# The order in which a decoder kernel's tensors lie in an SBUF partition

## What is computed

```python
def block(xb):                       # tokens; 8 heads, k = 16, 16384 experts a layer
    q = (xb @ w_query).reshape(tb, PEER_HEADS, 2, PEER_KEY_DIM // 2)
    s = jnp.einsum('thpd,pnd->thpn', q, sub_keys)
    top_s, top_i = lax.top_k(s, k)
    cand_s = top_s[:, :, 0, :, None] + top_s[:, :, 1, None, :]
    ...
    gate = jax.nn.softmax(best_s, axis=-1)
    u = expert_u[idx]
    act = jax.nn.gelu(jnp.einsum('thkd,td->thk', u, xb))
    w = (gate * act)
    return jnp.einsum('thk,thkd->td', w, expert_v[idx])
```

## The kernel before

| tensor | bytes | starts before | starts after |
|---|---|---|---|
| h, hn, hT | 12288 each | 128 | 0 |
| gain, qT, skT, con | 4096, 8192, 2048, 2632 | 128 | 0 |
| wring | 32768 | 224 | 0 |
| arena | 77824 | 224 | 0 |
| gws | 40512 | 224 | 96 |
| small | 256 | 288 | 128 |
| g1w, rows512, onorm, feat_cols | 512, 2048, 1024, 88 | 32 | 160 |
| top | 128 | 128 | 384 |
| top_i, top_f, pairs and what follows | | unchanged | unchanged (pairs 0) |

## Time and profile before

### The profile page before, as it was taken

One profiled execution on the slowest core, in us unless ns is written; L12 is line 12 of the kernel. 1 busy time (PEld: TensorE's weight loads), 2 busy tenths in 40 slices (PEclk: granted clock), 3 DMA queues, 4 the chain that ended last, 5 costly groups with the idle time before them and its releaser, 6 DMA issues.

```text
span 1687.8 us, 13940 instructions
## 1 busy us (share of the span) xinstructions
PE 1402.9 (83%) x4006; PEld 672.1 (40%) x4006; DVE 1110.3 (66%) x2844; ACT 426.0 (25%) x1115; POOL 553.7 (33%) x582
## 2 busy tenths in 40 slices
PE   8999799799887779798788769797788878777785
PEld 7744454264333334343335324343335333333332
DVE  1233565767777786766867687776867677777764
ACT  1132122222332223321222223321222222222221
POOL 0023232234333332232433333242433434333331
PEclk9989899899999989899999989898999998999998
DMA  7500579999999999999999999999999999999994
GB/s 260 204 1 1 223 300 412 409 375 383 419 420 419 420 393 379 360 413 390 419 410 417 413 390 413 413 409 379 420 409 418 405 417 420 420 419 421 419 414 198
DMA packets 107953, 617.11 MB, mean 366 GB/s; under 512 B 10939, under 2 KB 11195, under 8 KB 40294
## 3 DMA queue, kind: packets, MB, share of 16 engines
q0 software_dynamic: 76032, 553.68, 80.1%
q1 hardware_dynamic: 31846, 62.53, 10.1%
HBM read 615.13 MB, written 1.05 MB: 365 GB/s over the span
## 4 chain that ended last, share of the span: by engine, by line
PE 46%; DMA 31%; DVE 12%; issue 6%; ACT 2%; POOL 1%; DVEq 0%; SPq 0%; POOLq 0%
DMA arena<-peer_uv,idx 31%; PE bank L1061 24%; PE bank L688 9%; DVE arena L1834 3%; PE bank L727 3%; PE bank L1036 3%; ACT arena L1393 1%; PE bank L857 1%; PE bank L877 1%; POOL arena L637 1%; DVE wgt L1855 1%; DVE pairs L1758 1%; DVE top_i L1768 1%; DVE top_i L1759 0%; DVE h L1840 0%
## 5 line engine op out<-in xcount | busy, mean ns | idle before, releaser
L1061 PE MATMUL bank<-arena 128*128 128x512 f32 x1944 | 956.8, 641 | 243.2 <-ACT arena L1393 220.3
L1834 DVE CUSTOM_DVE_ANT_0 arena<-arena,bank 128x1024 f32<-128x1024 f32 x528 | 639.7, 1219 | 369.7 <-DMA arena<-peer_uv,idx 366.1
L637 POOL DMA_INDIRECT arena<-peer_uv,idx x528 | 513.6, 973 | 946.0 <-PE bank L1061 907.5
L1061 PEld LDWEIGHTS bank<-arena 128*128 128x128 f32 x1944 | 381.7, 204 | 770.9 <-issue 743.9
L1393 ACT ACTIVATE arena<-con,wgt 128x128 f32<-128x128 f32 x486 | 170.7, 394 | 751.4 <-DVE wgt L1855 736.3
L688 PE MATMUL bank<-wring,hT 128*128 128x512 f32 x368 | 162.9, 596 | 0.0
L1382 ACT ACTIVATE gl<-dots 128x2 f32<-128x2 f32 x264 | 53.6, 203 | 284.8 <-DVE dots L1834 279.2
L688 PEld LDWEIGHTS bank<-wring,hT 128*128 128x128 f32 x368 | 70.8, 193 | 89.5 <-issue 89.5
L1855 DVE SCALAR_TENSOR_TENSOR wgt<-gate_e,z,gl 128x2 f32<-128x2 f32 x264 | 57.5, 218 | 25.6 <-ACT gl L1382 19.5
L1840 DVE SCALAR_TENSOR_TENSOR h<-arena,wgt,h 128x1024 f32<-128x1024 f32 x42 | 54.0, 1285 | 1.7 <-DVE wgt L1855 0.2
L1382 ACT ACT_TABLE_LOAD x39 | 50.0, 1283 | 0.7
(11 more groups left out here) (209 smaller groups left out, 899.5 us busy)
## 6 DMA issues: line engine op xcount, KB each, us to landing
wring<-gla_w_in SPq DMA_DIRECT2D x12, 2048.0 KB
arena<-peer_uv,idx POOLq DMA_INDIRECT x528
wring<-gla_w_out SPq DMA_DIRECT2D x4, 2048.0 KB
wring<-peer_w_query SPq DMA_DIRECT2D x4, 2048.0 KB
wring<-attn_w_by_tile SPq DMA_DIRECT2D x3, 2048.0 KB
gws<-peer_w_query SPq DMA_DIRECT2D x2, 2048.0 KB, 13.6
wring<-attn_w_out_by_pair SPq DMA_DIRECT2D x2, 2048.0 KB
hn<-uq_by_kind SPq DMA_DIRECT2D x1, 1152.0 KB, 16.7
```

The costliest lines, as they stand in the source:

```text
L637: nc.gpsimd.indirect_dma_start(out=uvrow[:, n % RING, :], out_offset=None, in_=io["peer_uv"].rearrange("l e d -> (l e) d"), in_offset=bass ...
L1061: last = nc.tensor.matmul(yacc[:, 512 * i:512 * i + 512], wdiag[:, k % DIAGS, :], rows_of(g, k, 1)[:, 512 * i:512 * i + 512], start=first, ...
L1834: v.tensor_tensor_reduce(out=rows, in0=rows, in1=xnow, scale=1.0, scalar=0.0, op0=ALU.mult, op1=ALU.add, accum_out=dots[:, g % 2, k:k + 1] ...
```

## The change

Four tensors are declared first: `small` (256 bytes) and `top` (128), which together fill the 384 bytes up to a multiple of 512, then `arena` and `wring`. The rest follows in its old order. No instruction, DMA, wait or size is changed, and each tensor keeps its name and use.

```diff
+        small = sb("small", [P, 64])
+        top = sb("top", [P, 2, TOPK])
+        arena = sb("arena", [P, RING * 2 * D + DIAGS * P])
+        wring = sb("wring", [P, WSLOTS, KC * 512])
         h = sb("h", [P, NB, D])
         hn = sb("hn", [P, NB, D])
         hT = sb("hT", [P, KC, ROWS])
@@
         con = sb("con", [P, LIVE_CONSTS])
-        wring = sb("wring", [P, WSLOTS, KC * 512])
-        arena = sb("arena", [P, RING * 2 * D + DIAGS * P])
         gws = sb("gws", [P, 10128])
-        small = sb("small", [P, 64])
         g1w = sb("g1w", [P, KC, RANK])
@@
-        top = sb("top", [P, 2, TOPK])
         top_i = sb("top_i", [P, 2, TOPK], U32)
```

## The result

The changed kernel takes 1669.86 us (median of six runs, 1666.24 to 1673.69), the kernel before in the same sessions 1691.86 us (six runs): a ratio of 0.9873, 95% interval 0.9855 to 0.989, so 22 us less. The profiled execution took 1667.05 us, its span is 1664.9 us.

A forecast was written before the change was run, and what follows sets the result against it. DMA engines, busy throughout 240 to 1665 us, bound the kernel: startup, bytes over rate, short tail. All terms 0, so 1689.6 us plus 0, given as 1691 beside the runs' median; range 1672 to 1698.

The forecast's parts named there:

- rival B: Saturated gathers: the start costs 4.4 ns a row; 426 GB/s instead of 420, 15 us less, 1676 us; chance 16%.
- Step 1: Gathers' 8192-byte packets into arena: moving their start from 224 to 0 saves nothing; bounds -4.4 and +4.4 ns a row.
- straight line: DMA packets of 2048 to 8192 bytes at 224 or 128: 38 ns per KB plus a constant of 7.1 to 8.1 ns.
- comparison by rate: Packet times from GB/s of single-size stretches: constants at 224 and 128 differ by 0.3 ns, so alignment was put at 0.
- comparison with the aligned sub-keys: Startup sub-key load, 256-byte pieces at 0: 7.8 ns above payload against 10.4 for 2048-byte packets; alignment worth at most 2.6 ns.
- The first gathers: Gathers from 187 to 189 us, few queued: 426 GB/s, 307.7 ns a row against 312.1 saturated; difference laid to saturation.
- Step 2: 20 weight loads in the bound stretch, 1280 packets an engine: taken as 0, bounds -3.3 and +3.3 us.
- Rival A: DMA packets: bytes below the start cost like payload, 8.3 ns a gathered row; -38 us, 1653 us; chance 5%.
- cap of 435 GB/s: DMA ports: the skill page's ceiling would cap any gain of a saturated stretch at 3.4% of 420.
- Rival C: DMA writes meeting engines' accesses at the same place: slower, +4.4 ns a gathered row, +18 us, 1709 us; chance 8%.
- Rival D: Tensor placement: the change does not align, arena at another odd place; time the same, within the forecast, no separate chance.
- Steps 3, 4 and 5: Startup loads, VectorE's operands and PE's moving operands: 0 each; bounds 1.6 us for startup, 2.6 us for VectorE.

The follow-up runs named there:

- arena_only: Kernel before with only arena moved to 0 mod 512; wring and gws stay at 224, h to con at 128: 1673.5 us, ratio 0.9879.
- all_at_256: Changed kernel with arena, wring and h to con moved to 256 mod 512: 1669.3 us, ratio 0.9853 to the kernel before.
- wring_only: Kernel before with only wring moved to 0 mod 512; arena and gws stay at 224, h to con at 128: 1685.2 us, ratio 0.9961.
- all_at_32: Changed kernel with arena, wring and h to con moved to 32 mod 512: 1691.8 us, ratio 1.001 to the kernel before.
- rest_only: Kernel before with only h, hn, hT, gain, qT, skT and con moved to 0 mod 512: 1691.4 us, ratio 0.9995.
- gws_too: Changed kernel with gws at 0 mod 512 as well, con behind it: 1670.89 us, ratio 0.9876 to the kernel before.
- source_and_all_at_32: Changed kernel with arena, wring and h to con at 32 mod 512, and the weights' HBM rows 32 bytes past a multiple of 256: 1693.0 us, ratio 0.9996.
- all_at_64: Changed kernel with arena, wring and h to con moved to 64 mod 512: 1686.7 us, ratio 0.9967 to the kernel before.

## Why the prediction was wrong

The forecast, no change at 1691 us, failed, and the range ended at 1672, 2 us above the median. The mechanism is that of rival B, which had 16%: under pressure the start costs a few nanoseconds a row.

*Step 1, the gathers' packets, is where it fell: "It doesn't follow the start".* The straight line through the earlier trace rows was read rightly, but it could only exclude a price that grows with the bytes between boundary and start. A price that is the same for 224 and for 128 goes into the constant, and there it was, since all four sizes compared started off the boundary. The term for a row was put at 0, and it is 5.1 ns: from 240 us on the 8192-byte packets take 318.1 ns on the mean before and 313.0 in the changed kernel, and 4080 x 5.1 = 21 us. By rate it is the same. Rows at 427 GB/s (arena_only and all_at_256; the changed kernel has 425 to 428) are 8192 x 16 / 427 = 307.0 ns instead of 312.1, 5.1 less, and 2048-byte rows from 12 to 16 us are 79.9 ns at 410 GB/s instead of 84.7 at 387, 4.8 less. So about 5 ns for a packet, whatever its size from 2 to 8 KB, is the price of a start off 256 bytes. With 38 ns per KB taken off, the constants of aligned packets are 3.0 and 3.9 ns, where those of before are 8.1 and 8.7.

*The comparison with the aligned sub-keys* was the one that pointed right. By duration it had 7.8 ns above payload for an aligned packet and 10.4 for one at 224. In the changed kernel the 2048-byte packets from 12 to 16 us all take 84 ns, which is 8 above payload, so the 7.8 was good. The 2.6 ns between them was called the most that alignment could be worth and then put at 0, in favour of the comparison by rate, which had no aligned packet in it. And 2.6 was itself a mean over unlike parts. In the earlier trace rows I had taken 7 to 16 us as one stretch at 393 GB/s. Its two ends, in the kernel before:

```profile
DMA packets 590, 1.21 MB, mean 403 GB/s; under 512 B 0, under 2 KB 0, under 8 KB 590
...
DMA packets 756, 1.55 MB, mean 387 GB/s; under 512 B 0, under 2 KB 0, under 8 KB 756
```

The rate from 7 to 10 us says little by itself: over the profiles with 2048-byte loads it lies between 369 and 409 GB/s, whatever wring's start (382 in the changed kernel, 403 in wring_only). The packets' durations say more. Before, their median is 84 ns from 7 to 10 us, 86 from 10 to 12 and 88 from 12 to 16; in the changed kernel it is 84 throughout. So the extra time was not there at first, and the mean over the stretch hid part of it.

*The first gathers* were a sign of the same kind: 307.7 ns at the same start of 224 was put down to a short window, with "more queued work alone explains it". The packets bear the sign out: their median is 309 ns from 187 to 189 us, as in the changed kernel, against 313 from 450 to 600 us. But that 4.4 ns came so near to the price was in part luck. It rests on 2 us, in which one row more or less is 1% of the rate, and the changed kernel shows 410 GB/s in the same window where the kernel before shows 426. The prediction had named the point ("an address could matter only when the writes are pressed") and then weighed it at 16%.

*Rival B's sum* gave 15 us, 85% of 18, and 22 were measured. Its term for a row was 4.4 ns and is 5.1, and it came through whole instead of at 85%. Its missing term is the weights. *Step 2* put them at 0 with a bound of 3.3 us for their 1280 packets. Their own packets did stay inside it (0.8 ns each, 1.0 us), but the step left out that aligned weights make the gathers beside them quicker, which in wring_only is about 5 us. In the changed kernel those gathers are aligned themselves, so this is part of the 21 us above and is not counted again.

*Rival A* (bytes below the start cost like payload, 5%) falls by all_at_32, and its rates, 431 for gathers and 436 for weights, were never seen. (The 3.4% that the prediction gives for a cap of 435 GB/s is the share of the time; in rate it is 3.6% above 420.) The page DMA: Bandwidth & Descriptors of the Trainium skill, section How a descriptor splits into AXI transactions, names the boundary of 256 bytes, and the runs at 32, 64, 128 and 256 agree with that part. Its count of beats would charge 32 bytes one beat and 224 bytes seven; here they cost the same. In the page's table a descriptor of 576 bytes needs three transactions when it is aligned and four when it starts at 224; a fixed price for a packet is compatible with one transaction more, but no run here isolates that. I had held only the beats, and not the number of transactions, against the rows.

*Rival C* (slower) fell: the gathers went up to 427. *Rival D* too: the tensors are aligned as said. *Steps 3, 4 and 5* held: aligned startup loads gave no gain that can be seen (rest_only, gws_too), and VectorE's 1220 and 1285 ns and PE's 592 ns stayed. The reading of what bounds the kernel held as well: 22 us less of a DMA engine's time (21 in the gathers' packets, 1 in the weights') became 22 us less of the kernel's. Beside the mixers some slack stayed, as from 690 to 740 us:

```profile
690.00:740.00 50.00, 43.30 (x107) 20.22 (x106) 35.35 (x85) 11.20 (x29) 12.17 (x13) 0.87 0.93 373
```

The share there is 0.93 as in the earlier trace rows, at 373 GB/s instead of 369.

## What to carry over

Let every tensor that a long run of DMAs fills start at a multiple of 256 bytes in its partition: here it cost nothing but the order of the declarations, and it was worth about 5 ns for each packet while the DMA engines were the bound, 1.6% in a stretch of 8 KB rows alone and 6% in one of 2 KB rows alone. Where the two were mixed and the large rows lay off the boundary, aligning the small ones mainly sped up the large ones beside them. When the profile is to tell whether a property matters, look for a pair of rows in which it is absent in one and present in the other under the same load; a straight line through rows that all have it says nothing about it. And look at the two ends of a stretch before its mean rate is used: here the effect was absent at one and full at the other.

## What the runs showed of the hardware

For loads from HBM it is the start of the row in SBUF that sets this price: sources at 32 past a multiple of 256 left a load at 410 GB/s. Stores to HBM were not tried.

The extra time of a packet off the boundary is not there from the first packet, and there is no fixed delay. In source_and_all_at_32 and all_at_64 the 2048-byte packets have a median of 88 ns from 7 to 8 us already, some 2 us after these loads begin; in the kernel before it leaves 84 ns only after 10 us. A pause between transfers seems to let it go again: in the kernel before the gathers' packets have a median of 313 ns from 195 to 200 us, 309 from 200 to 230, where the DMA share is 0.81, and 313 in the full stretch from 450 us on. This is the manner of a backlog that has to fill first.

Whether a packet off the boundary pays also depends on those around it. The gathers at 224 took 316 ns in the median beside weights at 224 and 309 beside weights at 0. The 3 KB rows of `uq`, at 128 in both kernels, ran slowly behind wring's loads at 224 and quickly behind the same loads at 0. First the kernel before, then wring_only, from 17.2 to 18.2 us:

```profile
q1 hardware_dynamic: 129, 0.40, 101.7%
```

```profile
q1 hardware_dynamic: 136, 0.42, 102.8%
```

Before, 129 packets took 101.7% of 16 x 1000 ns, 126.1 ns each; behind an aligned wring 136 took 102.8%, 120.9 ns each. An aligned packet did not pay for those ahead of it: in rest_only, with `uq` at 0 behind wring at 224, the 3 KB packets take 121 ns in the median. That a backlog of writes is behind all this is inferred from these times, not measured.
